# Projections of a two-block sequence mixer: order of the dot products, a start by pieces, and an earlier weight split

## What is computed

```python
# each layer of the first block (l = 0, 1)
shift, scale, gate = split(silu(c) @ w_ada[l] + b_ada[l], 3)
hx = rms_norm(x, norm_g[l]) * (1 + scale) + shift
px = hx @ w_in[l]                 # input projection
y  = mixer(px) @ w_out[l]         # output projection, 1024 x 1024
x  = x + gate * y
# second block
shift, scale, gate = split(silu(c_2) @ w_ada_2 + b_ada_2, 3)
h = rmsnorm(x, norm_w_2) * (1 + scale) + shift
u = h @ w_in_2                    # last input projection
y = mixer_2(u) @ w_out_2          # last output projection, 2048 x 1024
out = rmsnorm(x + gate * y, final_norm_w_2)
```

## Time and profile before

| | us |
|---|---|
| median of 3 runs (4733.04 to 4744.11) | 4739.21 |
| the profiled execution | 4740.44 |
| its span, first to last instruction | 4738.8 |
| PE busy | 3926.3 (83%) |
| out0, first to last product (1289 to 1495) | 206 |
| out1 (2506 to 2690) | 184 |
| in_2 (2724 to 3645) | 921 |
| out_2 (4322 to 4721) | 399 |

### The profile page before, as it was taken

The page is one execution under the profiler, slowest core; times in us unless marked ns, Lnnn a source line. Parts: engine busy times, 40 slices in busy tenths (PEclk is TensorE's granted clock), DMA queues, the critical chain, the costliest instruction groups (busy, mean ns, idle before and its releaser), DMA issues. The chain is left out here.

```text
span 4738.8 us, 50755 instructions
## 1 busy us (share of the span) xinstructions
PE 3926.3 (83%) x18774; PEld 3161.0 (67%) x18774; DVE 2543.2 (54%) x3454; ACT 1617.0 (34%) x2665; POOL 1160.2 (24%) x969
## 2 busy tenths in 40 slices
PE   4659998688686899868868799999998967776998
PEld 1548887566475688656647578878886656664776
DVE  2635943688354495358845563440000479995554
ACT  2332102676221210157722222241111755553331
POOL 1421110122021111012202111111110048884444
PEclk7879999799897899979989899999999989997999
DMA  5342112321463312242126521132211365554443
GB/s 210 117 135 76 67 76 86 94 54 43 146 208 126 112 71 80 71 104 56 50 92 227 187 103 67 67 120 98 77 69 66 128 149 150 145 138 154 171 171 109
DMA packets 315775, 529.45 MB, mean 112 GB/s; under 512 B 26878, under 2 KB 203670, under 8 KB 299608
## 3 DMA queue, kind: packets, MB, share of 16 engines
q1 hardware_dynamic: 276970, 353.85, 24.6%
q0 software_dynamic: 38592, 172.82, 9.8%
HBM read 373.59 MB, written 153.00 MB: 111 GB/s over the span
## 5 line engine op out<-in xcount | busy, mean ns | idle before, releaser
L450 PE MATMUL in_ps<-h,in_wp 128*128 128x512 f32 x6624 | 1509.7, 390 | 18.6 <-POOL in_wp L613 18.6
L450 PEld LDWEIGHTS in_ps<-h,in_wp 128*128 128x128 f32 x6624 | 1247.4, 188 | 280.9 <-POOL in_wp L613 21.4
L1670 PE MATMUL out_ps<-out_y,out_wp 128*128 128x512 f32 x3072 | 727.5, 399 | 78.3 <-ACT out_y L1550 34.9
L1670 PEld LDWEIGHTS out_ps<-out_y,out_wp 128*128 128x128 f32 x3072 | 588.8, 192 | 216.9 <-issue 66.7
L583 DVE SCALAR_TENSOR_TENSOR cy<-cu,in_cw,cy 128x2048 f32<-128x2048 f32 x120 | 314.5, 2621 | 4.3
L1603 POOL TENSOR_TENSOR out_wp<-out_w,out_wp 128x2048 fp32r<-128x2048 f32 (+1 forms) x48 | 192.8, 4017 | 442.4 <-ACT out_wp L1539 442.4
L511 ACT ACTIVATE in_ob<-in_ps 128x2048 f32<-128x2048 f32 x37 | 69.7, 1885 | 663.6 <-PE in_ps L450 663.6
L998 DVE TENSOR_TENSOR att_pT<-att_T,att_pT 128x512 fp32r<-128x512 f32 x320 | 221.2, 691 | 91.2 <-ACT att_pT L923 87.5
L613 POOL TENSOR_TENSOR in_wp<-in_w,in_wp 128x1024 fp32r<-128x1024 f32 x75 | 200.8, 2679 | 253.3 <-ACT in_wp L461 217.7
L1932 DVE TENSOR_SCALAR hi_z<-hi_z 128x4 f32<-128x4 f32 x1 | 0.2, 170 | 461.8 <-ACT hi_z L1889 461.8
L977 DVE CUSTOM_DVE_ANT_0 att_S<-att_S,att_mk,att_nsink 128x640 f32<-128x640 f32 x256 | 226.2, 884 | 26.7 <-PE att_S L846 25.8
(11 more groups left out here) (491 smaller groups left out, 6539.0 us busy)
## 6 DMA issues: line engine op xcount, KB each, us to landing
in_w<-in_w_in SPq DMA_DIRECT2D x75, 512.0 KB, 3.6
gates<-in_ob POOLq DMA_DIRECT2D x36, 1024.0 KB, 4.2
out_w<-in_w_out SPq DMA_DIRECT2D x32, 1024.0 KB, 4.8
out_mw<-in_w_ada_rows SPq DMA_DIRECT2D x48, 512.0 KB, 3.9
att_qf<-q SPq DMA_DIRECT2D x64, 256.0 KB, 4.3
out_yr<-y SPq DMA_DIRECT2D x16, 1024.0 KB, 6.3
x<-out_x POOLq DMA_DIRECT2D x64, 256.0 KB, 3.2
out_yr<-y SPq DMA_DIRECT2D x32, 512.0 KB, 5.7
```

What stands on the lines that cost most here:

```text
L450: mm = nc.tensor.matmul(ps[:, q, c * W:(c + 1) * W], wp[:, q, i, k], h[:, j, k, c * W:(c + 1) * W], start=(n + k == 0), stop=(n == 2 and k ...
L1670: mm = nc.tensor.matmul(ps[:, u % NB, :W], wp[:, u % NW, a, k], y[:, c % 2, b, k], start=(i + k == 0), stop=(i == 2 and k == KY - 1))
```

## The change

- out0: `gather` comes before the dot products of its tile, in out1 as well. In out0 the row blocks get two buffers (`NMW`), so that SP loads one while DVE works on the other; the elementwise products, which nobody reads, go to two PSUM banks (`products`) instead of SBUF; results rotate through 4 PSUM banks instead of 5 (`NB`). A dot product now waits for the one before it.
- out_2: weight tile 1 is issued and taken up after the first piece instead of the last (`FIRST`). PE makes tiles 0 and 1 of chunk 0 together, piece by piece (`pieces`). From chunk 1 on ACT makes the squares of tiles 0, 1 and 2 together at tile 2 (`SQUARE_AT`).
- in_2: head and tail of weight tile 2 are made before the first tiles are emptied (`soon`).

The diff, cut to its core (the first `modulation` is SP's, the second DVE's; the piece that moves `weights(1)` stands on SP and on ACT; `pieces` is PE's):

```diff
@@ project @@
+        soon = decays
             def tile(it, q, *rest, last=False):
-                if ahead is not None and not last:
+                if ahead is not None and not last and not (soon and isinstance(it, int) and it == 0):
                     ahead(it + q, 1 - q)
...
                 ahead(0, 0)
+                if soon:
+                    ahead(0, 1)
+                    ahead(1, 0)
...
             def lead(it, q):
+                if soon and isinstance(it, int) and (it, q) == (1, 0):
+                    heads()
                 act.wait_ge(w_in[q], it * 16 + 16)
...
-                if isinstance(t, int) and t == 0:
+                if isinstance(t, int) and t == 0 and not soon:
                     heads()
@@ project_out @@
-    NB, SQ, S1, S2 = 5, 5, 6, 7
+    NB, SQ, S1, S2 = (4, 4, 5, None) if later and not middle else (5, 5, 6, 7)
+    FIRST, SQUARE_AT = (G, 0) if kept else (1, 2)
...
-            mw, mc = s.sb("mw", [P, D]), s.sb("mc", [P, m_n, D])
+            NMW = 1 if middle else 2
+            mw, mc = s.sb("mw", [P, NMW, D]), s.sb("mc", [P, m_n, D])
-            unused = s.sb("unused", [P, D], BF16) if m_n > 1 else None
...
+        products = s.ps("products", [P, 2 * CH]) if later and not middle else None
...
             def modulation(j):
-                wait(sp, dotted, j * m_n)
-                sp.dma_start(mw[:], m_w[j]).then_inc(mw_in, 16)
+                wait(sp, dotted, (j + 1 - NMW) * m_n)
+                sp.dma_start(mw[:, j % NMW], m_w[j]).then_inc(mw_in[j % NMW], 16)
...
             for p in range(G):
                 piece(0, p)
-            weights(1)
+                if p + 1 == FIRST:
+                    weights(1)
...
-                square(u)
+                if kept or c == 0 or n > SQUARE_AT:
+                    square(u)
+                elif n == SQUARE_AT:
+                    for v in range(u - SQUARE_AT, u + 1):
+                        square(v)
...
+            def pieces():
+                for p in range(G):
+                    for u in range(2):
+                        for i, (a, b) in enumerate(PARTS):
+                            if p == 0 and i < 2:
+                                pe.wait_ge((led, parted)[i], u + 1)
+                            if u == 0 and i != 1:
+                                pe.wait_ge((yled, None, yparted)[i], p + 1)
+                            for k in range(p * KP, (p + 1) * KP):
+                                mm = nc.tensor.matmul(ps[:, u, :W], wp[:, u, a, k], y[:, 0, b, k], start=(i + k == 0), stop=(i == 2 and k == KY - 1))
+                        if p == G - 1:
+                            mm.then_inc(mm_done, 1)
...
             def modulation(j):
...
                 for n in range(m_n):
-                    out = unused if n + 1 < m_n else mw
-                    nc.vector.tensor_tensor_reduce(out=out[:], in0=mw[:], in1=mc[:, n], scale=1.0, scalar=0.0,
+                    wait(dve, dotted, j * m_n + n)
+                    out = mw[:, j % NMW] if products is None else products[:]
+                    nc.vector.tensor_tensor_reduce(out=out, in0=mw[:, j % NMW], in1=mc[:, n], scale=1.0, scalar=0.0,
...
                 add(u)
+                gather(u)
                 if later and 0 <= u - LEAD < NJ:
                     modulation(u - LEAD)
                 if later and u - LEAD == NJ:
                     modulations_done()
-                gather(u)
```

More of the change, by code:

```diff
@@ L1461, in project_out @@
             m_cond, m_w, m_b, m_g, m_mod, m_gain, m_n, m_factor = later
-            mw, mc = s.sb("mw", [P, D]), s.sb("mc", [P, m_n, D])
+            NMW = 1 if middle else 2
+            mw, mc = s.sb("mw", [P, NMW, D]), s.sb("mc", [P, m_n, D])
             mb, mg = s.sb("mb", [P, NJ]), s.sb("mg", [P, KT])
-            unused = s.sb("unused", [P, D], BF16) if m_n > 1 else None
-            mw_in, mc_in, silued, dotted, modded = s.sem("mw_in"), s.sem("mc_in"), s.sem("silued"), s.sem("dotted"), s.sem("modded")
-        ps = s.ps("ps", [P, 8, CH])
+            mw_in = s.sems("mw_in", NMW)
+            mc_in, silued, dotted, modded = s.sem("mc_in"), s.sem("silued"), s.sem("dotted"), s.sem("modded")
+        ps = s.ps("ps", [P, S2 + 1 if middle else S1 + 1, CH])
+        products = s.ps("products", [P, 2 * CH]) if later and not middle else None
         w_in, y_in, x_in, stored = s.sems("w_in", 2), s.sems("y_in", 2), s.sems("x_in", KT * NX), s.sems("stored", KT * NX)
@@ L1658, in sums @@
                 mm.then_inc(summed, 1)
+            def pieces():
[10 more added lines that the diff above has]
+                            mm.then_inc(mm_done, 1)
             pe.wait_ge(const, 3 if middle else 2)
-            for u in range(U):
+            if not kept:
+                pieces()
+            for u in range(0 if kept else 2, U):
                 c, n = divmod(u, KT)
```

2 lines of the change are left out of this document (1 added, 1 removed).

## The result

The changed kernel takes 4688.6 us (median of 4 runs, 4683.6 to 4692.55), the kernel before on the same chip 4737.4 (4733.0 to 4744.1). The ratio is 0.9895, with a 95% interval from 0.9878 to 0.9912: 49 us less, 1.05%. The forecast of 4693 was 4.4 us too high. The profiled execution has a span of 4687.6 us, the one before 4738.8.

A forecast was written before the change was run, and what follows sets the result against it. PE leads, so only its idle or low-clock places in four stages can gain. 18.5 - 5.5 + 10.9 + 15.0 + 7.5 = 46.4 off 4740.4 gives 4694, median 4693; own range 4686 to 4702, full range 4679 to 4714.

The forecast's parts named there:

- out0, forecast 18.5: In out0, a second row-block buffer removes the 6.2 us loop and PE's waits: gain 18.5 us, bounds 13.5 and 18.8.
- DVE keeps up, and PE becomes the bound: In out0, DVE would need 42 us a chunk against PE's 44.75, so PE sets the pace.
- out1, forecast a loss of 5.5: In out1, the moved gather delays the single buffer's next load at data pieces: loss 5.5 us, bounds 0 and 9.
- the loop around a piece: In out1, the dot products around a data piece would be 9.5 us apart instead of 7.6.
- The upper bound of 9: In out1, the largest loss allowed, 9 us, with a wait at the second chunk's product by ones too.
- The rival that out1 keeps up: In out1, row blocks land sooner or the piece is issued earlier, the 5.5 us are not lost: 4687; chance 0.13.
- in_2, forecast 10.9: In in_2, PE's wait of 8.96 us for weight tile 2 and 1.9 us of low clock go; bounds 8 and 10.9.
- out_2, changes: forecast 15.0: At out_2's chunk changes, 12.9 us of waits for weight tile 3 and the low clock behind them go; bounds 9 and 15.
- out_2, start: forecast 7.5: At out_2's start, tiles 0 and 1 piece by piece end tile 2 at 4371.2 instead of 4378.8; bounds 10.6 and 0.
- A new wait in out0: In out0, the data piece or a slower queue sets DVE's pace, only 4 of 18.5 us come: 4707; chance 0.10.
- A dot product at half rate into PSUM: Dot products into PSUM take 2.75 us, costing 58 us, so the kernel is slower, 4751; chance 0.05.
- Start and changes giving less: In out_2, pieces or tile 5 come so late that 7.5 + 15.0 shrinks to 10: 4705; chance 0.10.

The follow-up runs named there:

- the run with the old order at out1's pieces: Changed kernel, with out1's gather behind the dot product only in tiles 2 and 5 of a chunk: 4679.0 us, ratio 0.9880 to the kernel before.
- the run with the buffers alone: Kernel before, with only out0's second row-block buffer, four banks and the target in PSUM: 4718.3 us, out0 187.0 us.
- the run with the old order: Changed kernel, with the gather behind the dot product again in all of out1: 4681.0 us, ratio 0.9885 to the kernel before, out1 185.0 us.
- the weight tile's head first: Changed kernel with out1's old order, and in out0 and out1 ACT makes the weight tile's head before the data piece's: 4672.1 us, ratio 0.9861 to the kernel before.

## Why the prediction was right, and where it was not

The time and the sign are right, and so is the mechanism in all five places. But that the sum came out at 46.4, the forecast's own number, is luck. Its terms are off by 2.2 and 0.7 (less gained), 3.9 (more lost), and 5.0 and 1.8 (more gained), which cancel; two of them, out1 and the changes of out_2, lie outside the bounds that they were given. The means of the second table give the same picture. 4 us of the measured difference are none of the change's.

**out0, forecast 18.5, measured 16.3, 17.6 by the means.** The step "DVE keeps up, and PE becomes the bound" is right (44.43 us from one product by ones to the next, 44.75 forecast). The target in PSUM didn't change the dot product's rate (1.23 us; I took 1.28). Its accumulator is read in 0.14 us instead of 0.08, and the second of a tile starts 1.32 us after the first. That isn't the target's doing alone: behind the second dot product, with the same target, the next operation starts after 1.15 us. The 0.17 stand only where one dot product waits for the other; the forecast had 0.1 for that wait. DVE's reserve hides it. What is missing in the changed kernel's profile is chunk 0's last row: 64 products in 17.06 us, where other executions have 14.8. One of these is the run with the old order at out1's pieces, whose out0 is the changed kernel's:

```profile
1342.58 14.80 PE L1702 MATMUL out_ps<-out_y,out_wp 128*128 128x512 f32 x64 [1.46 <-POOL out_wp L1619]
```

The windows say what it is (length, PE busy with its count, granted clock, DMA share and GB/s): the changed kernel, then the run with the buffers alone, which also has 14.8.

```profile
1340.00:1348.50 8.50, 8.45 (x27) 0.71 0.52 166
```

```profile
1340.70:1348.50 7.80, 7.75 (x34) 1.00 0.54 178
```

Of four executions with the same out0, two have this row at 14.8 us and two at 16.9 and 17.1, behind waits that look alike (1.8 to 2.1 us, then 0.7 to 1.5). So 2.2 us of the shortfall are the low clock in this execution; what decides whether it falls there, no run shows. With the waits gone (the weight tile's head first) the granted clock was 1.00 from 1336 to 1352 in one such run.

**out1, forecast a loss of 5.5, measured 9.4.** The mechanism was right, and the run with the old order shows it. The step that was mis-sized is the loop around a piece, 9.5 us by the forecast. The changed kernel has 10.4, 10.7, 10.7 and 9.7. The piece of the rows above was issued at 2571.72, ACT began its head at 2579.38 and DVE the split at 2581.33, 9.6 us after the issue, where the forecast took 8.1. Over four pieces of the changed kernel ACT begins 6.2 to 7.7 us after the issue, in the profile before 6.1 to 6.5; the piece with 6.2 has the loop of 9.7, near the forecast. With 0.7 us more a piece the reserve of 1.2 us at the second chunk was gone too (1.34 us of wait), a wait of 1.58 came at a data piece beside the 3.49, and there was low clock behind the 3.49. The upper bound of 9 had a wait at the second chunk in it, and was still a little short. 0.7 us of the 9.4 are not the order's: they lie in chunk 0 and are in the run with the old order too (59.9 us from the first product to the first product by ones, 59.8 with the change, 59.1 before). The rival that out1 keeps up is out.

**in_2, forecast 10.9, measured 10.2**, 10.4 by the means. The tail of weight tile 3 was ready 0.7 us before PE needed it, 1.5 by the forecast. No wait.

**out_2, changes: forecast 15.0, measured 20.0.** The waits, 12.9 us, went as foreseen, and tile 5 was never late. The mis-sized term is what lies behind them. I divided the row ahead of the wait, 22.37 us by its 96 products, and got 0.233 a product, by which the rows behind were only 1.2, 0.6 and 0.4 us too long. The undisturbed row of the changed kernel corrects this: 384 products in 87.65 us. From the two, a product takes (87.65 - 22.37) / 288 = 0.2267 us, and a row that follows another has 0.6 us more, whatever its length. (The rows of out0 confirm it: 192 x 0.2267 + 0.6 is 44.1.) A row behind a wait has only 0.3 more: 44 products in 10.28 us, 64 in 14.80. So the three rows of before, 68.32, 67.66 and 56.28 us for 288, 288 and 240 products, were 2.7, 2.1 and 1.6 us too long, and each of the three cuts cost another 0.3 (22.37 us and, at the full rate, 65.6 make 88.0; the row in one piece takes 87.65). That is 7.3 us instead of 2.2, and 12.9 + 7.3 is the measured 20. The first of these rows in the trace of before (length, then PE, PEld, DVE, ACT and POOL busy, granted clock, DMA):

```profile
4471.57:4539.80 68.23, 68.23 (x289) 56.23 (x290) 39.21 (x33) 24.02 (x27) 32.47 (x7) 0.96 0.44 154
```

The granted clock is 0.96 over the row; 4% of 68.2 is 2.7 us, the same as by the count.

**out_2, start: forecast 7.5, measured 9.3**, 8.4 by the means. Weight tile 1's head began 13.0 us after the stage's first load (SP at 4289.79, ACT at 4302.77), 2 us sooner than I had it, and all behind it came sooner. Piece 1's split is the row on which the forecast rested:

```profile
4304.86 4.51 POOL L1619 TENSOR_TENSOR out_wp<-out_w,out_wp 128x2048 fp32r<-128x2048 f32 x1 [3.51 <-ACT out_wp L1550]
```

```profile
4307.84 2.74 DVE L1725 SCALAR_TENSOR_TENSOR out_y<-out_yr,y_gain,out_y 128x512 fp32r<-128x512 f32 x2 [5.28 <-ACT out_y L1561]
4311.16 1.42 DVE L1725 SCALAR_TENSOR_TENSOR out_y<-out_yr,y_gain,out_y 128x512 fp32r<-128x512 f32 x2 [0.58 <-ACT out_y L1561]
```

The split takes 2.74 us beside POOL's tail and 1.42 without it. The tail ends at 4309.37, the split at 4310.58, 1.21 later: it moved little until the tail was over. By the rule of the Trainium skill (SBUF — State Buffer, section Who interferes with whom) the first of the two operations waits for the end of the GpSimd instruction; the rows agree. The block was real, but 1.3 us instead of the 4.6 that I let it cost, since the piece reached DVE late in POOL's tail. The last split ended 4.2 us later than before, not 6.4.

**The rivals.** A new wait in out0: none. A dot product at half rate into PSUM: 1.23 us, so this one is out, and with it the only case that ended slower. Its sums were off: (44.75 - 8 x 2.2 - 4.6) / 16 is 1.41 us, not 1.53, and even from 1.53 the point where 48 dot products eat up the forecast's gain of 46 us is 2.5 us, not 2.7. Start and changes giving less: they gave 7 us more.

**What stays open.** The later data pieces in out1: in the changed kernel ACT takes up three of four pieces 6.9 to 7.7 us after their issue. With the gather behind, nine executions have 32 of 36 pieces at 5.9 to 6.7, but the other four at 7.1 to 9.0. So a late piece also comes without the early gather, only more rarely; SP issues the same loads in the same order around it, and the next row block's load 4.6 to 5.1 us behind it in both. The new order in out1 was profiled once, and no run separates DVE's, POOL's and the queues' part. And 4 us of the whole lie in stages without a change.

## What to carry to other kernels

A single buffer that is refilled when its last reader ends makes a loop out of everything that stands ahead of that reader on its engine. Before an instruction is moved ahead of such a reader, ask if the loop has the time; the same move was free with two buffers and cost 9 us with one. In an in-order engine, work for later that waits for a transfer must not stand ahead of work for now: one swap on ACT gave 4 to 7 us in out0 (against the three other runs with out0 as changed) and 1 us in out1. And a rate must be taken from the difference of two rows of different length: a short row divided by its count has its end in it, and hides the low clock that one wants to price.

## What the runs showed of the hardware

- A DVE dot product of two SBUF operands of 1024 float32 columns takes 1.22 to 1.23 us with its elementwise target in PSUM, as in SBUF; only the read of the accumulator is longer, 0.14 us against 0.08.
- Behind short waits of TensorE the granted clock can differ from execution to execution of the same stage (0.71 over 8.5 us of out0 in the changed kernel, 1.00 in other runs), at a cost of 2.2 us. A wait of 1.82 us was enough in out_2 before the change: the 240 products behind it took 56.28 us, 1.6 above the rate. A stage without such waits gains more than their length, and scattered less here: out0 took 181.5 and 181.1 us in the two runs without them, and 185.9 to 189.6 in four with them.
